# Residual norms of the second row tile in column halves, first loads reordered, waits for half the transposes, last norm interleaved

## The chip, the cores and the metric

One core of a Trainium2 chip runs the whole program as one launch. The metric is device time in microseconds (us). The kernel before took 3188.24 us (median of 3 runs, 3188.09 to 3198.32). Its profiled execution took 3180.1 us, of which the span of the core's instructions is 3178.1 us.

## The reference, cut to what matters

Two transformer stacks run one after the other on 256 tokens of width 1024, all in float32. The first has four layers, the second two.

```
first_block, layer i of 4 (kind = i % 3):
    q, k, v, ... = split(x @ w_in[kind]);  mix = attention of that kind;  mo = attention over memory rows
    x = layer_norm(ALPHA * x + concat(mix, mo) @ w_out[i])
    x = layer_norm(ALPHA * x + (silu(x @ w_gate) * (x @ w_up)) @ w_down)         # D_FF = 2816
second_block, layer i of 2:
    mix = mixer_ab(h) if i == 0 else mla(h)
    h = layer_norm(DN_ALPHA * h + mix)
    h = layer_norm(DN_ALPHA * h + mem_cross_attention(h, mem))
    h = layer_norm(DN_ALPHA * h + hier_moe(h))    # 32 experts of 1024 x 512 x 3 weights, 2 per token
layer_norm(x) = (x - mean) * rsqrt(var + eps) * g + b, over the 1024 columns
```

So there are fifteen norms with their gain and bias: one of the memory rows, twelve after a residual sum with a linear's output, and two after the experts.

## The kernel before, in words

The 256 rows are two tiles of 128 partitions, t = 0 and t = 1. The activations live in `x` (128 x 2 x 1024). TensorE (PE) takes them transposed, as `xT`, so each norm is followed by eight 128x128 transposes of a tile into PSUM (`trp`, two banks, four transposes a bank; function `x_columns`), and ScalarE (ACT) copies each bank to `xT`. `await_transposes` makes PE wait until all copies are done.

Weights come through a ring of 12 slots of 1 MB (`ring`), in the order in which SyncE (SP) issues them. PE frees a slot by an increment of `slots_used` at the last matmul that reads it, and SP, which waits in order, then issues the load twelve places on. In the expert stages six more slots in the arena join the ring, so 18 MB can be on their way; each stage reads 192 pieces of 1 MB.

The order on each engine is written out by hand; nothing is scheduled. Engines meet at semaphores. The places that matter here:

- The start: SP issues `ident`, `x` (both tiles in one DMA), the memory rows, the causal mask, two small tables and then the weights. PE waits for `ident` and `x`, does 16 transposes, waits for their copies, and starts the first projection (`linear_chunk`), whose weights are the first pieces in the ring.
- A residual norm (`add_and_normalise`, 12 of them): PE finishes tile 0 of a linear (`pe_for_vec`), goes on with tile 1, and puts tile 0's transposes shortly before tile 1's last matmuls. VectorE (DVE) adds PSUM to `x` over 1024 columns, does two `bn_stats` of 512 columns and one `bn_aggr`, asks GpSimd (POOL) for the inverse root, subtracts and multiplies by the gain meanwhile, waits for the root and does the last multiply-add, which ends in `ln_done`. It does the same for tile 1 when all the linear's slots are free (`slots_used >= complete`). Tile 1's transposes on PE stand behind whatever work can run without it.
- That work is: after the feed-forward of a layer (`ffn`), the next layer's first two chunks for tile 0 (`linear_by_tile`, four times); after attention in layers 0 to 2 and after `mla`, the next memory projection (`next_memory_kv`); after `mixer_ab`, a memory projection; after attention in layer 3, nothing; after cross attention (twice), only the router's small matmuls for tile 0 (`moe`).
- In `ffn` the down products of the last three of 11 units are held, so that tile 0 ends twelve matmuls before tile 1. For tile 1 they run unit by unit, the two 512-column halves of the output side by side.
- After the experts (`moe` on DVE) both tiles are normalised one after the other; after the last one SP writes `out` in one DMA.

## Time and profile before

| | |
|---|---|
| median of 3 runs | 3188.24 us |
| profiled execution | 3180.1 us |
| its span | 3178.1 us |
| PE busy (matmul) | 2769.9 us, 87% |
| DVE busy | 667.2 us, 21% |
| ACT busy | 382.4 us, 12% |
| POOL busy | 99.0 us, 3% |
| DMA, mean over the span | 221 GB/s |

The span cut in 40 slices shows two kinds of stages. In most slices PE is busy 90% or more and the DMA engines move 80 to 190 GB/s. In the two expert stages (slices 25 to 30 and 34 to 39) it is the other way round: about 420 GB/s, and PE at 60 to 80%. An engine's idle time costs something only where the engine that sets the end waits for it, so the rows below are read one place at a time: a view of idle times by releaser first, then the timeline around each place. In the rows a float32 matmul is recorded as two MATMUL rows, so x36 stands for 18 matmuls.

### The profile page before, as it was taken

How to read it: one execution, taken by the hardware profiler on the slowest of the kernel's cores; microseconds unless marked ns; L12 is line 12 of the kernel's file. 1: busy time of each engine (PE TensorE's matmuls, PEld its weight loads, DVE VectorE, ACT ScalarE, POOL GpSimd, SP SyncE). 2: the span in 40 equal slices, each digit the busy share in tenths (PEclk: the TensorE clock that was granted, in tenths of full speed). 3: DMA queues.
4: the chain of work that ended last, by engine and by line, in shares of the span. 5: the costliest groups of instructions: out<-in, count | busy, mean ns of one | idle time of the engine just before them, and what ended most of it. 6: DMA issues, size and time to landing. Idle time of an engine off the chain costs nothing.

```text
span 3178.1 us, 30120 instructions
## 1 busy us (share of the span) xinstructions
PE 2769.9 (87%) x12918; PEld 1655.7 (52%) x12918; DVE 667.2 (21%) x1611; ACT 382.4 (12%) x733; POOL 99.0 (3%) x48
## 2 busy tenths in 40 slices
PE   8999999999999999899999998766767998766664
PEld 4567755677457764577647775222223655322221
DVE  2610013000140013500155503100101323110111
ACT  1300002000120001300021112000000312000000
POOL 1000000000000000000000100000000000000000
PEclk9999999999999999999999998877788998888887
DMA  7344443544525444344423244999999435899996
GB/s 286 106 147 146 159 137 112 181 147 133 172 88 169 149 130 159 103 137 148 148 88 136 80 151 185 413 422 421 421 421 359 146 122 190 366 421 421 421 421 287
DMA packets 245464, 703.21 MB, mean 221 GB/s; under 512 B 18651, under 2 KB 119513, under 8 KB 195923
## 3 DMA queue, kind: packets, MB, share of 16 engines
q1 hardware_dynamic: 244032, 699.43, 58.8%
q8 instruction: 106, 1.74, 0.2%
q10 hardware_dynamic: 1299, 1.83, 0.2%
q14 instruction: 27, 0.22, 0.0%
HBM read 698.33 MB, written 1.05 MB: 220 GB/s over the span
## 4 chain that ended last, share of the span: by engine, by line
issue 73%; PE 13%; DMA 10%; POOL 2%; SPq 1%; DVE 1%; ACT 0%; ACTq 0%; POOLq 0%; DVEq 0%
PE sco L685 7%; PE lin L685 6%; DMA arena<-in_moe_w_down 3%; DMA arena<-in_moe_w_gate 3%; DMA ring<-in_moe_w_up 2%; DMA ring<-in_moe_w_gate 2%; DMA ring<-in_moe_w_down 2%; POOL roots L2003 2%; SPq L529 1%; PE trp L685 0%; PE trp L797 0%; ACT arena L1614 0%; DVE x L2071 0%; DVE arena L2637 0%; POOLq L179 0%
## 5 line engine op out<-in xcount | busy, mean ns | idle before, releaser
L685 PE MATMUL lin<-ring,arena 128*128 128x512 f32 (+4 forms) x3340 | 1183.2, 584 | 45.8 <-DMA arena<-in_moe_w_down 21.8
L685 PEld LDWEIGHTS lin<-ring,arena 128*128 128x128 f32 (+2 forms) x3340 | 518.5, 174 | 623.9 <-issue 597.2
L685 PE MATMUL sco<-arena,ring 128*128 128x256 f32 (+1 forms) x2836 | 621.5, 380 | 9.7 <-DVE arena L2594 9.0
L685 PEld LDWEIGHTS sco<-arena,ring 128*128 128x128 f32 x2836 | 541.5, 192 | 98.9 <-issue 16.7
L685 PE MATMUL sco<-ring,arena 128*32 128x512 f32 (+2 forms) x1428 | 276.8, 817 | 169.2 <-DMA ring<-in_moe_w_gate 89.2
L685 PE MATMUL sco<-arena 128*32 128x512 f32 (+6 forms) x1360 | 240.1, 595 | 95.4 <-DMA arena<-in_moe_w_gate 45.5
L685 PE MATMUL lin<-arena 128*128 128x128 f32 (+9 forms) x1632 | 257.7, 394 | 19.8 <-DMA ring<-in_moe_w_down 9.0
L685 PEld LDWEIGHTS sco<-ring,arena 128*32 128x32 f32 (+1 forms) x1428 | 79.5, 154 | 338.7 <-issue 334.7
L685 PEld LDWEIGHTS sco<-arena 128*32 128x32 f32 (+4 forms) x1360 | 103.7, 163 | 205.4 <-issue 189.9
L2240 DVE TENSOR_TENSOR arena<-arena,sco 128x256 f32<-128x256 f32 x88 | 37.1, 421 | 822.5 <-ACT arena L1701 822.5
L2003 POOL TENSOR_TENSOR roots<-roots 128x8 f32<-128x8 f32 x42 | 98.6, 2350 | 3072.8 <-DVE roots L2048 3044.5
L685 PEld LDWEIGHTS lin<-arena 128*128 128x128 f32 (+4 forms) x1632 | 144.0, 164 | 92.9 <-issue 68.2
L2655 DVE TENSOR_TENSOR arena<-arena,sco 128x512 f32<-128x512 f32 x16 | 11.0, 688 | 745.1 <-PE sco L685 745.1
L685 PE MATMUL lin<-arena,ring 128*128 128x256 f32 (+2 forms) x648 | 131.6, 385 | 3.6 <-issue 2.9
L1701 ACT ACTIVATE arena<-sco 128x256 f32<-128x256 f32 x88 | 33.8, 384 | 790.4 <-PE sco L685 790.4
L1614 ACT ACTIVATE arena<-trp 128x512 f32<-128x512 f32 (+1 forms) x123 | 67.0, 590 | 469.6 <-PE trp L797 466.9
L685 PEld LDWEIGHTS lin<-arena,ring 128*128 128x128 f32 (+1 forms) x648 | 108.8, 181 | 26.1 <-issue 7.3
L2082 DVE SCALAR_TENSOR_TENSOR x<-x,lin 128x1024 f32<-128x1024 f32 x24 | 29.3, 1222 | 217.2 <-PE lin L685 217.2
L685 PEld LDWEIGHTS trp<-arena 128*128 128x128 f32 x512 | 62.6, 203 | 16.6 <-issue 16.6
L685 PE MATMUL trp<-arena 128*128 128x128 f32 x512 | 65.6, 290 | 4.7 <-DVE arena L2637 4.7
L1605 ACT ACTIVATE arena<-lin 128x1024 f32<-128x1024 f32 (+3 forms) x36 | 32.9, 913 | 284.2 <-PE lin L685 284.2
L2167 DVE RECIPROCAL arena<-lin 128x256 f32<-128x256 f32 x34 | 59.7, 1756 | 9.4 <-PE lin L685 8.6
(249 smaller groups left out, 1116.3 us busy)
## 6 DMA issues: line engine op xcount, KB each, us to landing
ring<-in_moe_w_down SPq DMA_DIRECT2D x92, 1024.0 KB, 26.9
ring<-in_w_gate_up SPq DMA_DIRECT2D x88, 1024.0 KB, 5.1
ring<-in_moe_w_gate SPq DMA_DIRECT2D x88, 1024.0 KB, 26.9
ring<-in_moe_w_up SPq DMA_DIRECT2D x80, 1024.0 KB, 27.0
arena<-in_moe_w_up SPq DMA_DIRECT2D x48, 1024.0 KB, 26.7
ring<-in_w_down SPq DMA_DIRECT2D x44, 1024.0 KB, 4.8
arena<-in_moe_w_gate SPq DMA_DIRECT2D x40, 1024.0 KB, 27.2
arena<-in_moe_w_down SPq DMA_DIRECT2D x36, 1024.0 KB, 27.3
```

The costliest lines, as they stand in the source:

```text
L529: sp.dma_start(slot_rows(s).rearrange("p (k n) -> p k n", k=src.shape[1]), src).then_inc(slot_full[s], 16)
L685: return nc.tensor.matmul(o, lhsT, rhs, start=start, stop=stop)
L1605: nc.scalar.activation(dst[:, :, lo:lo + n], lin[:, pair:pair + 2, 0:n], ACT.Copy).then_inc(proj_done, 1)
L1614: nc.scalar.activation(dst, trp[0:rows, b, 0:n].rearrange("p (a b) -> p a b", a=shape[1]), ACT.Copy, scale=scale).then_inc(tr_done, 1)
L1701: nc.scalar.activation(silu_g[:, f, :], sco[:, f, 0:SEQ], ACT.Silu).then_inc(silu_done, 1)
L2003: nc.gpsimd.tensor_tensor(root_out[:, b, :], root_in[:, b, :], root_power, ALU.pow).then_inc(root_done, 1)
L2082: V.scalar_tensor_tensor(x[:, t, :], x[:, t, :], alpha, lin[:, 2 * t:2 * t + 2, :].rearrange("p a b -> p (a b)"), ALU.mult, ALU.add).then_ ...
L2167: V.reciprocal(pair_rinv, bank[:, SEQ:2 * SEQ]).then_inc(dve_step, 1)
L2240: V.tensor_tensor(hT[:, u % 4, f, :], silu_g[:, f, :], sco[:, f, SEQ:2 * SEQ], ALU.mult).then_inc(h_done, 1)
L2655: V.tensor_tensor(pair_h, pair_silu, sco[:, 1, :], ALU.mult).then_inc(h_done, 1)
```

## The change

Five things are changed.

1. Start. `x` comes in two DMAs, one a tile, with a semaphore of its own for tile 1; the first weight chunk (two slots) is issued right behind them, ahead of the memory rows, the mask and the small tables.
2. Residual norms of tile 1 (12). The add is cut in two halves of 512 columns, each with its `bn_stats` behind it; the first half starts when PE has finished that half's columns (two slots fewer than `complete`, or an extra increment of `pe_for_vec` in `ffn`), the second when all is done. For the latter, `ffn` does tile 1's held products half by half: all units for columns 0 to 511, then all units for the rest. Its three held slots are all freed in the second half.
3. Waits for half the transposes. In `linear_by_tile` and at the router, PE waits for the first of tile 1's two copies and does k = 0 to 3; before k = 4 it waits for the second.
4. The norms after the experts (2). Statistics and root requests of both tiles come first, then the two subtract-multiplies, then the two multiply-adds.
5. `out` is written in two DMAs, one a tile, each when its tile is done.

The core of the diff:

```diff
@@ -549,7 +549,9 @@
             sp.dma_start(ident[:, :], const("ident")).then_inc(x_loaded, 16)
-            sp.dma_start(x[:, :, :], A["x"][0].rearrange("(t p) d -> p t d", p=P)).then_inc(x_loaded, 16)
+            sp.dma_start(x[:, 0, :], A["x"][0, 0:P, :]).then_inc(x_loaded, 16)
+            sp.dma_start(x[:, 1, :], A["x"][0, P:2 * P, :]).then_inc(second_tile_loaded, 16)
+            load_chunk(A["w_in_a"][0], *FIRST_CHUNKS[0][0])
             sp.dma_start(memrows, A["mem"][0].rearrange("(t p) d -> p t d", p=P)).then_inc(input_loaded, 16)
@@ -557,7 +559,7 @@
                 w_in = (A["w_in_a"], A["w_in_b"], A["w_in_c"])[kind][j]
-                for c, n in FIRST_CHUNKS[kind][:3]:
+                for c, n in FIRST_CHUNKS[kind][int(layer == 0):3]:
                     load_chunk(w_in, c, n)
@@ -642,9 +644,10 @@
                 load_ln(A["ln3_g_2"][layer], A["ln3_b_2"][layer])
-            sp.wait_ge(ln_done, NT * LAYER_NORMS)
-            sp.dma_start(out[0].rearrange("(t p) d -> p t d", p=P), x[:, :, :]).then_inc(out_written, 16)
-            sp.wait_ge(out_written, 16)
+            for t in range(NT):
+                sp.wait_ge(ln_done, NT * LAYER_NORMS - NT + 1 + t)
+                sp.dma_start(out[0, t * P:(t + 1) * P, :], x[:, t, :]).then_inc(out_written, 16)
+            sp.wait_ge(out_written, 16 * NT)
         @block.tensor
@@ -734,9 +737,11 @@
                 between()
-                await_transposes()
+                await_transposes(1)
                 for i, (pair, n, w) in enumerate(head):
                     for k in range(kt):
+                        if i == 0 and k == 4:
+                            await_transposes()
                         last = mm(lin[:, pair + 1, 0:n], srcT[:, k, P:2 * P], w[k // 4][:, k % 4, :], start=k == 0, stop=k == kt - 1)
@@ -815,8 +820,8 @@
                     transposes([x[:, t, (b + j) * P:(b + j + 1) * P] for j in range(4)], free_slots if b == 0 else 0)
-            def await_transposes():
-                pe.wait_ge(tr_done, tr_items[0])
+            def await_transposes(but=0):
+                pe.wait_ge(tr_done, tr_items[0] - but)
             def cross_scores(h):
@@ -1002,12 +1007,17 @@
                 last.then_inc(pe_for_vec, 1)
-                for u in held:
-                    for f in range(2):
-                        if u == held[-1] and f == 1:
-                            x_columns(0)
-                        last = products(u, rows[u], f, 1)
-                    last.then_inc(slots_used, 1)
+                for n in range(2):
+                    for u in held:
+                        for f in range(2):
+                            if n == 1 and u == held[-1] and f == 0:
+                                x_columns(0)
+                            last = mm(lin[:, 2 + n, :], hT[:, u % 4, f, P:2 * P], rows[u][:, f, n * 512:(n + 1) * 512],
+                                      start=u + f == 0, stop=u == FFN_UNITS - 1 and f == 1)
+                        if n == 1:
+                            last.then_inc(slots_used, 1)
+                    if n == 0:
+                        last.then_inc(pe_for_vec, 1)
             def linear_columns(srcT, chunks, between=None, inside=None):
@@ -1303,9 +1313,11 @@
                         x_columns(1, 1)
-                        await_transposes()
+                        await_transposes(1)
                     o = sco[:, 0, t * 64:t * 64 + 36]
                     for k in range(KD):
+                        if t == 1 and k == 4:
+                            await_transposes()
                         mm(o, xT[:, k, t * P:(t + 1) * P], w[:, k, :], start=k == 0, stop=False)
@@ -1439,6 +1451,8 @@
             for t in range(NT):
+                if t:
+                    pe.wait_ge(second_tile_loaded, 16)
                 for b in range(0, KD, 4):
@@ -2062,6 +2076,11 @@
                 dve.wait_ge(dve_step, t_step.next())
+                scaled(rows, t, s, dst)
+
+            def scaled(rows, t, s, dst=None):
+
+                dst = rows if dst is None else dst
                 V.bn_aggr(mean_var[:, t, :], bn[:, t, :]).then_inc(dve_step, 1)
@@ -2071,18 +2090,33 @@
                                        ALU.mult, ALU.add).then_inc(ln_done, 1)
-            def add_and_normalise(alpha):
+            def add_and_normalise(alpha, projected=True):
                 complete = used.n
                 s = own_slot(2)
-                for t in range(NT):
-                    if t == 0:
+                dve.wait_ge(pe_for_vec, t_pe.next())
+                V.scalar_tensor_tensor(x[:, 0, :], x[:, 0, :], alpha, lin[:, 0:2, :].rearrange("p a b -> p (a b)"),
+                                       ALU.mult, ALU.add).then_inc(y_taken, 1)
+                dve.wait_ge(y_taken, t_taken.next())
+                normalise(x, 0, s)
+                for h in range(2):
+                    half = x[:, 1, 512 * h:512 * h + 512]
+                    if h == 1:
+                        dve.wait_ge(slots_used, complete)
+                    elif projected:
+                        dve.wait_ge(slots_used, complete - 2)
+                    else:
                         dve.wait_ge(pe_for_vec, t_pe.next())
+                    ins = V.scalar_tensor_tensor(half, half, alpha, lin[:, 2 + h, :], ALU.mult, ALU.add)
+                    if h == 0:
+                        ins.then_inc(dve_step, 1)
+                        dve.wait_ge(dve_step, t_step.next())
                     else:
-                        dve.wait_ge(slots_used, complete)
-                    V.scalar_tensor_tensor(x[:, t, :], x[:, t, :], alpha, lin[:, 2 * t:2 * t + 2, :].rearrange("p a b -> p (a b)"),
-                                           ALU.mult, ALU.add).then_inc(y_taken, 1)
-                    dve.wait_ge(y_taken, t_taken.next())
-                    normalise(x, t, s)
+                        ins.then_inc(y_taken, 1)
+                        dve.wait_ge(y_taken, t_taken.next())
+                    last = V.bn_stats(bn[:, 1, h * 6:h * 6 + 6], half)
+                last.then_inc(dve_step, 1)
+                dve.wait_ge(dve_step, t_step.next())
+                scaled(x, 1, s)
             def rotate(heads, cos, sin, half, scratch=rope_tmp, dst=None):
@@ -2690,8 +2724,22 @@
                 s = own_slot(2)
-                for t in range(NT):
-                    normalise(moe_sum, t, s, x)
+                rstd = []
+                for t in range(NT):
+                    for h in range(2):
+                        last = V.bn_stats(bn[:, t, h * 6:h * 6 + 6], moe_sum[:, t, h * 512:(h + 1) * 512])
+                    last.then_inc(dve_step, 1)
+                    dve.wait_ge(dve_step, t_step.next())
+                    V.bn_aggr(mean_var[:, t, :], bn[:, t, :]).then_inc(dve_step, 1)
+                    dve.wait_ge(dve_step, t_step.next())
+                    rstd.append(ask_root(mean_var[:, t, 1:2], ALU.add, LN_EPS))
+                for t in range(NT):
+                    ins = V.scalar_tensor_tensor(x[:, t, :], moe_sum[:, t, :], mean_var[:, t, 0:1], ring[:, s, 0:D], ALU.subtract, ALU.mult)
+                ins.then_inc(dve_step, 1)
+                dve.wait_ge(dve_step, t_step.next())
+                for t in range(NT):
+                    dve.wait_ge(root_done, t_root.next())
+                    V.scalar_tensor_tensor(x[:, t, :], x[:, t, :], rstd[t], ring[:, s, D:2 * D], ALU.mult, ALU.add).then_inc(ln_done, 1)
             V.memset(ones[:, :], 1.0).then_inc(dve_step, 1)
@@ -2794,7 +2842,7 @@
                 passed(3 * FFN_UNITS)
-                add_and_normalise(ALPHA)
+                add_and_normalise(ALPHA, False)
             for layer in range(SECOND_LAYERS):
```

On SP, at the start of the program. Before:

```order
L551 DMA ident<-in_consts 128x128
L552 DMA x<-in_x 128x2x1024
L553 DMA arena<-in_mem 128x2x1024
L554 DMA causal<-in_consts 128x512
L555 DMA small<-in_consts 128x8
L556 DMA ints<-in_positions 128x2
L448 DMA ring<-in_w_in_a 128x4x512 x2
L448 DMA ring<-in_w_in_a 128x4x328 x2
```

And now:

```order
L551 DMA ident<-in_consts 128x128
L552 DMA x<-in_x 128x1024
L553 DMA x<-in_x 128x1024
L448 DMA ring<-in_w_in_a 128x4x512 x2
L555 DMA arena<-in_mem 128x2x1024
L556 DMA causal<-in_consts 128x512
L557 DMA small<-in_consts 128x8
L558 DMA ints<-in_positions 128x2
L448 DMA ring<-in_w_in_a 128x4x328 x2
```

The two loads of the first weight chunk have moved ahead of four others, and `x` has become two loads.

On DVE, tile 1 of the norm behind the first attention (`x` and `lin` are the residual and PE's result, `small` the statistics, `roots` the inverse root). Before:

```order
L2082 SCALAR_TENSOR_TENSOR x<-x,lin 128x1024 [waits slots_used]
L2062 BN_STATS small<-x 128x6 [waits y_taken]
L2062 BN_STATS small<-x 128x6
L2065 BN_AGGR small<-small 128x2 [waits dve_step]
L2048 TENSOR_SCALAR roots<-small 128x1 [waits dve_step]
L2068 SCALAR_TENSOR_TENSOR x<-x,small,ring 128x1024
L2071 SCALAR_TENSOR_TENSOR x<-x,roots,ring 128x1024 [waits root_done,dve_step]
```

And now:

```order
L2109 SCALAR_TENSOR_TENSOR x<-x,lin 128x512 [waits slots_used]
L2116 BN_STATS small<-x 128x6 [waits dve_step]
L2109 SCALAR_TENSOR_TENSOR x<-x,lin 128x512 [waits slots_used]
L2116 BN_STATS small<-x 128x6 [waits y_taken]
L2084 BN_AGGR small<-small 128x2 [waits dve_step]
L2062 TENSOR_SCALAR roots<-small 128x1 [waits dve_step]
L2087 SCALAR_TENSOR_TENSOR x<-x,small,ring 128x1024
L2090 SCALAR_TENSOR_TENSOR x<-x,roots,ring 128x1024 [waits root_done,dve_step]
```

One add and one `bn_stats` of 512 columns now stand ahead of the wait for the linear's end.

On DVE, the last norm of the program (both tiles). Before:

```order
L2062 BN_STATS small<-arena 128x6 [waits slot_full6]
L2062 BN_STATS small<-arena 128x6
L2065 BN_AGGR small<-small 128x2 [waits dve_step]
L2048 TENSOR_SCALAR roots<-small 128x1 [waits dve_step]
L2068 SCALAR_TENSOR_TENSOR x<-arena,small,ring 128x1024
L2071 SCALAR_TENSOR_TENSOR x<-x,roots,ring 128x1024 [waits root_done,dve_step]
L2062 BN_STATS small<-arena 128x6 x2
L2065 BN_AGGR small<-small 128x2 [waits dve_step]
L2048 TENSOR_SCALAR roots<-small 128x1 [waits dve_step]
L2068 SCALAR_TENSOR_TENSOR x<-arena,small,ring 128x1024
L2071 SCALAR_TENSOR_TENSOR x<-x,roots,ring 128x1024 [waits root_done,dve_step]
```

And now:

```order
L2730 BN_STATS small<-arena 128x6 [waits slot_full6]
L2730 BN_STATS small<-arena 128x6
L2733 BN_AGGR small<-small 128x2 [waits dve_step]
L2062 TENSOR_SCALAR roots<-small 128x1 [waits dve_step]
L2730 BN_STATS small<-arena 128x6 x2
L2733 BN_AGGR small<-small 128x2 [waits dve_step]
L2062 TENSOR_SCALAR roots<-small 128x1 [waits dve_step]
L2737 SCALAR_TENSOR_TENSOR x<-arena,small,ring 128x1024 x2
L2742 SCALAR_TENSOR_TENSOR x<-x,roots,ring 128x1024 [waits root_done,dve_step]
L2742 SCALAR_TENSOR_TENSOR x<-x,roots,ring 128x1024 [waits root_done]
```

Tile 1's statistics have moved ahead of tile 0's two passes over the rows.

## Rows read from the trace of the kernel before

**Rows 1.** The page, part 1: busy time of each engine, share, instructions.

```profile
PE 2769.9 (87%) x12918; PEld 1655.7 (52%) x12918; DVE 667.2 (21%) x1611; ACT 382.4 (12%) x733; POOL 99.0 (3%) x48
```

**Rows 2.** Waits of PE over the span: releaser, us in total, times, longest.

```profile
PE trp L797 <- DVE x L2071: 17.6, 3, 7.2
PE lin L685 <- ACT arena L1614: 9.3, 11, 1.6
```

**Rows 3.** Stretches in the first expert stage: busy by engine, clock, DMA share, GB/s.

```profile
1980.00:1985.00 5.00, 4.31 (x41) 2.50 (x44) 0.00 (x0) 2.48 (x3) 0.00 (x0) 1.00 0.01 3
...
2010.00:2400.00 390.00, 252.95 (x1521) 89.60 (x1524) 39.11 (x114) 24.41 (x38) 0.00 (x0) 0.79 1.01 421
```

**Rows 4.** Timeline of the start: start, us, engine, line, operation, idle before.

```profile
6.47 3.78 PE L797 MATMUL trp<-ident,x 128*128 128x128 f32 x16 [6.47 <-DMA x<-in_x]
...
10.29 0.60 ACT L1614 ACTIVATE arena<-trp 128x512 f32<-128x512 f32 x1 [0.26 <-PE trp L797]
...
13.41 38.23 PE L685 MATMUL lin<-ring,arena 128*128 128x512 f32 x96 [3.16 <-DMA ring<-in_w_in_a]
```

**Rows 5.** DMA issues at the start: size, us from issue to landing.

```profile
x<-in_x SPq DMA_DIRECT2D x1, 1024.0 KB, 5.2
arena<-in_mem SPq DMA_DIRECT2D x1, 1024.0 KB, 7.4
```

**Rows 6.** Stretches where the clock changes; the column behind POOL is the clock.

```profile
13.00:14.00 1.00, 0.59 (x2) 0.37 (x3) 0.00 (x0) 0.00 (x0) 0.00 (x0) 0.94 1.05 389
...
17.00:18.00 1.00, 1.00 (x3) 0.38 (x2) 0.00 (x0) 0.00 (x0) 0.00 (x0) 0.85 1.07 374
...
1354.00:1356.00 2.00, 2.00 (x8) 1.65 (x7) 0.00 (x0) 0.00 (x0) 0.00 (x0) 0.67 0.00 0
```

**Rows 7.** Timeline, feed-forward of layer 0 into layer 1.

```profile
428.52 15.62 PE L685 MATMUL lin<-ring,arena 128*128 128x512 f32 x36
...
443.98 1.04 PE L797 MATMUL trp<-ident,x 128*128 128x128 f32 x8
...
444.61 1.09 ACT L1614 ACTIVATE arena<-trp 128x512 f32<-128x512 f32 x2 [15.24 <-PE trp L797]
...
445.75 2.84 PE L685 MATMUL lin<-ring,arena 128*128 128x512 f32 x6 [0.74 <-ACT arena L1614]
```

**Rows 8.** Timeline, tile 1 of the norm behind layer 3's attention.

```profile
1339.36 1.22 DVE L2082 SCALAR_TENSOR_TENSOR x<-x,lin 128x1024 f32<-128x1024 f32 x1 [7.45 <-PE lin L685]
...
1341.94 0.21 DVE L2065 BATCH_NORM_AGGREGATE small<-small 128x2 f32<-128x12 f32 x1
...
1346.47 1.97 PE L797 MATMUL trp<-ident,x 128*128 128x128 f32 x8 [7.15 <-DVE x L2071]
```

**Rows 9.** Timeline, second half of the router in the first expert stage.

```profile
1960.46 1.97 PE L797 MATMUL trp<-ident,x 128*128 128x128 f32 x8 [5.22 <-DVE x L2071]
...
1962.46 0.60 ACT L1614 ACTIVATE arena<-trp 128x512 f32<-128x512 f32 x1 [0.26 <-PE trp L797]
...
1963.11 3.63 PE L685 MATMUL sco<-ring,arena 128*128 128x36 f32 x16 [0.69 <-ACT arena L1614]
```

**Rows 10.** Timeline of the end.

```profile
3162.19 1.29 DVE L2062 BATCH_NORM_STATS2 small<-arena 128x6 f32<-128x512 f32 x2 [0.25 <-DVE arena L2645]
...
3163.99 2.60 POOL L2003 TENSOR_TENSOR roots<-roots 128x8 f32<-128x8 f32 x1 [479.55 <-DVE roots L2048]
...
3172.41 1.28 DVE L2071 SCALAR_TENSOR_TENSOR x<-x,roots,ring 128x1024 f32<-128x1024 f32 x1 [1.60 <-POOL roots L2003]
3173.73 0.40 SPq L646 DMA_DIRECT2D out<-x  x1
```

**Rows 11.** The DMA that writes the result: size, us to landing.

```profile
out<-x SPq DMA_DIRECT2D x1, 1024.0 KB, 4.0
```

**Rows 12.** DVE groups by shape: busy us, mean ns of one, idle before.

```profile
L2062 DVE BATCH_NORM_STATS2 small<-x 128x6 f32<-128x512 f32 x48 | 30.9, 685 | 0.8
...
L2465 DVE TENSOR_TENSOR arena<-arena,sco 128x512 f32<-128x512 f32 x16 | 11.0, 685 | 5.7 <-PE sco L685 5.6
```

More of the change, by code:

```diff
@@ L352, in build @@
         slots_used = sem("slots_used")
-        x_loaded, input_loaded = sem("x_loaded"), sem("input_loaded")
+        x_loaded, second_tile_loaded, input_loaded = sem("x_loaded"), sem("second_tile_loaded"), sem("input_loaded")
         proj_done = sem("proj_done")
```

## The prediction

> **What bounds the kernel now.** I read the page first: PE is busy 87% of the span, DVE, ACT and POOL far less [rows 1]. So outside the expert stages a microsecond counts only where PE stands still. Next the view of PE's waits, which gives the size of the prey. PE waits for a norm (DVE's last pass over x) 17.6 us in three places, and 9.3 us in eleven for ACT's copies of transposes [rows 2]. I went to each place in the timeline. The three waits for a norm are 7.15 us behind layer 3's attention [rows 8] and twice 5.2 us at the routers (what is left of the 17.6). In the other nine residual norms PE has other work until tile 1 is ready, so a shorter norm is worth nothing there.
>
> Then the stretches around the first expert stage. From 2010 to 2400 the DMA engines move 421 GB/s at full share, so the stage lasts as long as its weights. But ahead of it, from 1980 to 1985, they move 3 GB/s at 1% share [rows 3]: the slots are full, and the loads go on only when PE frees the first. The stage's end thus moves with PE's start, as long as that hole is not used up. The ends of the program are chains of their own: PE waits for x at the start [rows 4], and DVE, POOL and one DMA run alone at the end [rows 10].
>
> **The start.** Before, x lands at 1.19 + 5.2 = 6.4 us, the 16 transposes begin at 6.47, the last copy ends at 10.29 + 0.60 = 10.89, and PE then waits until 13.41 for weights [rows 4, 5]. The memory rows land at 1.66 + 7.4 = 9.06, so 1 MB takes 2.66 us here [rows 5]. Now tile 0 is half of x and lands 1.3 us earlier, at 5.1; tile 1 lands at 6.4 as before, sooner than PE has finished tile 0. The transposes shift as a block, and the last copy ends at 9.6. The first weight piece follows x and lands at 6.4 + 2.7 to 2.9 = 9.1 to 9.3. PE starts at 9.64 instead of 13.41: 3.8 us. The second piece lands near 12, and eight matmuls on the first take over 7 us. The memory rows' norm waits for its gain and bias, which stay behind the same number of bytes, and PE comes to it only after the 38 us of matmuls in rows 4.
>
> The clock comes on top. At 13.41 it was at its full 2.4 GHz; it fell to half at 13.9 and returned at 17.3 (0.94 and 0.85 are the means over 13 to 14 and 17 to 18 [rows 6]). Ahead of the fall PE had been idle since 10.25. That stretch cost 3.4 / 2 = 1.7 us. In the new order PE pauses only about 0.7 us between transposes and matmuls. I take it that the clock comes up at about 10.5, as it must have before, since nothing ran between 10.25 and 13.41, and doesn't fall: 0.4 us lost instead of 1.7. Start: 3.8 + 1.3 = 5.1 us. If the clock comes up only behind a stretch of matmuls as long as the one that ended at 17.3 (3.9 us), 1.9 us are lost instead of 1.7 and the start gives 3.5. A late return (6.2 us, as behind layer 3) would leave 2.4. If PE never falls and is fast at once, 5.5.
>
> The Trainium skill bears on just this. "TensorE: Matmul & The Clock Gate", Part 4 (PE-mode transpose), says that transposes do not count as work for the clock. By that rule the start would be worth the 3.5 above. Here the trace speaks against it, as the clock was full at 13.41 with nothing but transposes before [rows 6].
>
> **Waits for half the transposes.** In linear_by_tile the transposes end at 443.98 + 1.04 = 445.02, the second copy at 445.70, and PE goes on at 445.75, 0.74 us later [rows 7]. A copy takes 0.60 [rows 9], so the first ends at 445.21, and PE can go on at 445.26: 0.49 us. Four matmuls of 0.86 us (18 in 15.62 [rows 7]) cover the second copy. Four such places: 2.0 us. At a router the copies are 0.85 us apart at the half clock: the first is done before PE's last transpose ends (1960.46 + 1.97 = 1962.4), and the matmuls start at 1963.11 [rows 9]: 0.65 us each, 1.3 for two. Between them the four matmuls take 0.9, as 16 rows of k take 3.63; the second copy ends at 1963.06, in time.
>
> **Column halves.** Behind PE's last matmul DVE now adds 512 columns instead of 1024 and does one bn_stats instead of two. Before, from the add's start to bn_aggr: 1341.94 - 1339.36 = 2.58 us [rows 8]. Now an operation of 512 columns from PSUM takes 0.69 and a bn_stats 0.69 [rows 12], with two hand-overs of 0.03: 1.43. Gain 1.15 us where PE waits: layer 3 and two routers, 3.45 us. In the other nine places nothing. The first half's add costs nothing, since DVE idles until PE's end (7.45 us in rows 8). The idle of PE shrinks from 7.15 to 6.0, so the clock, which was at half there and came back at 1355.3 (0.67 over 1354 to 1356 [rows 6]), will still fall; how soon it returns varies between the 3.4 us at the start and 6.2 here. I put 0.3 us for it, with -0.5 and +1.4 as ends; the gathers at the two routers, which lie across the same rise, -1 to +1.
>
> **The expert stages** pass on what the router gains (0.65 + 1.15 = 1.8 us each), because the hole of over 5 us in the DMA stream [rows 3] stays open. The norm of the first expert stage is followed by a memory projection on PE, so its interleaving gives nothing.
>
> **The end.** Before, bn_stats begins at 3162.19, the last pass ends at 3172.41 + 1.28 = 3173.69 [rows 10]. Now: root 0 runs on POOL from 3163.99 as before; tile 1's statistics end at about 3165.4, the two subtract passes (1.28 each) at 3168.0, the first multiply-add at 3169.3. Root 1 can start only when root 0 is through, at 3166.6, and is done at 3169.2, just in time; the last pass ends at 3170.6. Gain 3.1 us. The result's 1 MB takes 4.0 us from issue to landing [rows 11]; at 1 MB in 2.66 us, half of it is 1.3 us shorter, and tile 0's half is under way by then: 1.2 us. End: 4.3 us, with 3.1 as the lower end if two DMAs finish no sooner than one.
>
> **Held products and slots.** By halves, ffn's held matmuls are as many as before, and each has its own weight load either way. The first held slot comes free after 8 of 12 matmuls instead of 4, 3.4 us later, the second 1.7. The load that takes it is used only after four chunks, over 40 us of PE's work. Cost nothing.
>
> **Sum.** 5.1 + 2.0 + 1.3 + 3.45 + 0.3 + 4.3 = 16.4 us. 3180.1 - 16.4 = 3163.7 for the profiled execution. That lay 0.26% under the median of the runs; scaled to 3188.24 it is 3172. In ratio 0.9948.
>
> **Rivals.**
> A. The clock at the start behaves as in the second case, and layer 3's return falls badly (-0.5): the sum is 14.0, and the time 3174. For it speaks that the first 16 transposes ran at the slow pace, 3.78 us, while 8 take 1.04 at the full clock and 1.97 at half [rows 4, 7, 8]; against it the full clock at 13.41. The Trainium skill's rule on transposes, cited above, is for this case.
> B. The clock comes back early at layer 3 (+1.4) and the gathers gain: 18 to 19 us, 3169.
> C. The expert stages swallow everything ahead of them, since they end with their DMA. Then only the last norm and the result are left: 4.3 us, 3184. Against it stands the hole at 1% share [rows 3], which must be gone for this; it holds where the DMA stream starts at a time of its own.
> D. Slower: the later slots. Loads go out in order, so each of the four feed-forward ends would push all loads behind it by 3.4 us. If PE came to the next layer's chunk just as it lands, it would wait 3.4 us four times, and each such idle would bring down the clock (1.7 to 3.1 us more): 20 to 26 us, against 16 gained. The kernel would be 4 to 10 us slower, 3192 to 3198. It decides once a load has under 3.4 us to spare. Only waits of PE for weights in the first four layers would speak for it, and I found one alone, at 13.41 [rows 4].
> E. The new order of loads does not hold PE's start earlier, because the two weight pieces land with the rest: the start gives 1.3 (tile 0) or nothing, sum 11 to 12.5, 3176.
>
> **Chances.** The forecast 0.40, A 0.27, B 0.13, C 0.05, D 0.04, E 0.11. A measurement of this kernel tells about 0.5% (16 us) from no change, and the forecast lies right on that line. Faster by over 0.5% are a bit over half of the forecast's own and B, and a share of A by the spread of the runs, 0.42; within 0.5% the rest with C and E, 0.54; slower by over 0.5% hardly D, 0.04. The range: B's end below and C above are 3169 and 3184, and the runs before spread by 10 us, which I add below in part: 3162 to 3184.
>
> **What would show it.** Start: first transposes at 5.1, first matmul at 9.6, clock not at half after 11. linear_by_tile: a gap of 0.2 to 0.3 us instead of 0.74. Layer 3: 6.0 us of idle; routers: 4.1 us, then no 0.69 us gap. Expert stage: the hole in the DMA stream a bit shorter, 421 GB/s as before, its end earlier by all that came before it. End: last pass 8.4 us after the first bn_stats instead of 11.5. Wrong if the hole is gone, if PE waits for weights in layers 1 to 3, or if POOL's second root ends later than the second subtract pass.

## The result, and the profile after

| us | before | after |
|---|---|---|
| median of the runs, five each | 3188.24 (3188.09 to 3198.32) | 3172.54 (3167.57 to 3176.57) |
| profiled execution | 3180.1 | 3170.12 |
| its span | 3178.1 | 3168.3 |
| mean granted clock of the span | 0.931 | 0.930 |

The ratio is 0.9939, with a 95% interval of 0.9918 to 0.9959: the kernel is faster by about 0.6%. A repetition of the same two kernels (e6_again below) gave 0.9968, 0.9949 to 0.9987. In that session the 23 runs of before fell into two groups, 13 at 3177.8 to 3180.8 us and 10 at 3193.9 to 3197.4, so a median depends on how many of each a session has. The means of all runs differ by 19.6 us in the first session (3191.9 and 3172.3) and by 12.2 in the repetition (3186.7 and 3174.5). The median came out where the prediction had it. The profiled execution did not: it gained 10.0 us where the sum said 16.4. The last part of this section is about that difference.

The places are read as before, one at a time. The start, in the timeline (columns: start, us, engine, line, operation, idle before), answers to [rows 4]:

```profile
4.95 3.56 PE L802 MATMUL trp<-ident,x 128*128 128x128 f32 x16 [4.95 <-DMA x<-in_x]
...
9.19 36.56 PE L688 MATMUL lin<-ring,arena 128*128 128x512 f32 x96 [0.69 <-ACT arena L1628]
```

The DMA issues of the start, for [rows 5]:

```profile
x<-in_x SPq DMA_DIRECT2D x2, 512.0 KB, 4.1
arena<-in_mem SPq DMA_DIRECT2D x1, 1024.0 KB, 11.0
```

The first matmul is at 9.19 instead of 13.41 (4.2 us), and its group of 96 rows takes 36.56 instead of 38.23 (1.7 us). The wait for weights, 3.16 us before, is gone; PE waits 0.69 us for a copy. Together 5.9 us, where the prediction had 5.1.

linear_by_tile between layers 0 and 1, for [rows 7]:

```profile
438.08 1.04 PE L802 MATMUL trp<-ident,x 128*128 128x128 f32 x8
438.71 1.09 ACT L1628 ACTIVATE arena<-trp 128x512 f32<-128x512 f32 x2 [15.24 <-PE trp L802]
439.36 1.98 PE L688 MATMUL lin<-ring,arena 128*128 128x512 f32 x4 [0.25 <-ACT arena L1628]
```

The wait is 0.25 us instead of 0.74, so 0.49, as forecast. The norm behind layer 3's attention, for [rows 8]:

```profile
1333.96 0.69 DVE L2109 SCALAR_TENSOR_TENSOR x<-x,lin 128x512 f32<-128x512 f32 x1 [6.12 <-PE lin L688]
1334.69 0.69 DVE L2116 BATCH_NORM_STATS2 small<-x 128x6 f32<-128x512 f32 x1
1335.42 0.21 DVE L2084 BATCH_NORM_AGGREGATE small<-small 128x2 f32<-128x12 f32 x1
...
1339.96 1.97 PE L802 MATMUL trp<-ident,x 128*128 128x128 f32 x8 [6.03 <-DVE x L2090]
1342.61 9.75 PE L688 MATMUL sco<-arena,ring 128*128 128x256 f32 x36 [0.69 <-ACT arena L1628]
```

From the last add's start to `bn_aggr` it is 1.46 us instead of 2.58, and PE stands still for 6.03 instead of 7.15. The clock comes back sooner too. Stretches of 2 us (columns: stretch, length, busy time by engine, then behind POOL the clock, DMA share, GB/s), for the last row of [rows 6]:

```profile
1344.00:1346.00 2.00, 2.00 (x6) 1.59 (x5) 0.00 (x0) 0.00 (x0) 0.00 (x0) 0.50 0.40 162
1346.00:1348.00 2.00, 2.00 (x10) 1.74 (x10) 0.00 (x0) 0.00 (x0) 0.00 (x0) 0.97 0.00 0
```

It is at 1.2 GHz up to 1346 and at 2.4 GHz from there, 3.5 us behind the first matmul at 1342.61, where before it took 6.2. The first router, second half, for [rows 9]:

```profile
1958.38 1.97 PE L802 MATMUL trp<-ident,x 128*128 128x128 f32 x8 [4.10 <-DVE x L2090]
1960.19 3.63 PE L688 MATMUL sco<-ring,arena 128*128 128x36 f32 x16
...
1968.73 2.35 PE L688 MATMUL sco<-arena,ring 128*128 128x32 f32 x10 [4.48 <-DVE arena L2628]
1973.42 5.79 PE L688 MATMUL trp<-arena 128*128 128x128 f32 x32 [2.35 <-DVE arena L2671]
1979.90 1.50 PE L688 MATMUL sco<-ring,arena 128*32 128x512 f32 x12 [0.69 <-ACT arena L1887]
```

The wait for the norm is 4.10 us instead of 5.22 and the 0.69 behind the transposes is gone. From the router's first matmul to the experts' first it is 27.7 us here and was 29.4; at the second router 27.6 and was 30.2. The two waits give 1.8 us at each; the rest is the gather of the routed rows (`trp<-arena`), 5.79 us for 5.54 at the first router and 5.67 for 6.31 at the second. The rows in between show what is still left: 4.48, 2.35 and 0.69 us of idle, and matmuls at half pace. In the expert stage the hole in the DMA stream stands as before, and behind it the 421 GB/s, for [rows 3]:

```profile
1979.00:1984.00 5.00, 4.31 (x42) 1.35 (x45) 0.00 (x0) 1.88 (x2) 0.00 (x0) 1.00 0.01 3
2010.00:2400.00 390.00, 253.74 (x1524) 89.47 (x1524) 39.07 (x114) 23.36 (x37) 0.00 (x0) 0.79 1.01 421
```

The end, for [rows 10, 11]: DVE, POOL and SyncE in the timeline, and the DMA that writes the result (size, us to landing).

```profile
3156.85 1.29 DVE L2730 BATCH_NORM_STATS2 small<-arena 128x6 f32<-128x512 f32 x2 [0.25 <-DVE arena L2679]
3158.65 4.24 POOL L2017 TENSOR_TENSOR roots<-roots 128x8 f32<-128x8 f32 x2 [477.85 <-DVE roots L2062]
3160.11 2.47 DVE L2737 SCALAR_TENSOR_TENSOR x<-arena,small,ring 128x1024 f32<-128x1024 f32 x2
3162.62 2.48 DVE L2742 SCALAR_TENSOR_TENSOR x<-x,roots,ring 128x1024 f32<-128x1024 f32 x2
3163.93 1.53 SPq L649 DMA_DIRECT2D out<-x  x2
```

```profile
out<-x SPq DMA_DIRECT2D x2, 512.0 KB, 2.7
```

From the first `bn_stats` to the last pass's end it is 8.25 us and was 11.50; from there to the span's end 3.2 and was 4.4. That is 4.45 us, against 4.3 forecast.

**Where the other microseconds went.** I took the start of tile 0's residual add at each of the twelve norms in both traces. The distance between the two traces is how far the kernel after is ahead at that point: 5.9 us at the first and second norm, 4.4 at the third and fourth, 4.9 at the fifth and sixth, 5.4 at the seventh, 7.9 at the eighth, 1.0 at the ninth and tenth, 2.5 at the last two, then 5.3 at the last norm and 9.8 at the end. It should never fall, and it falls twice: by 1.5 us between the second and the third (layer 1's attention), and by 6.9 between the eighth and the ninth (`mixer_ab`). The second of these stretches, before and after:

```profile
1569.74:1805.67 235.93, 224.21 (x1363) 156.47 (x1362) 136.13 (x223) 43.31 (x74) 15.76 (x8) 0.96 0.26 89
```

```profile
1561.88:1804.71 242.83, 231.94 (x1363) 162.65 (x1362) 136.58 (x223) 43.50 (x74) 15.76 (x8) 0.92 0.25 87
```

PE has the same 1363 matmul rows and DVE the same 136 us. Only the clock differs, 0.96 and 0.92. With one linear_by_tile in it the stretch should have become 0.5 us shorter, and it is 6.9 longer. Layer 1's attention, before and after, tells the same in small (clock 0.99 and 0.97):

```profile
419.30:547.30 128.00, 122.18 (x485) 66.14 (x484) 38.02 (x96) 25.23 (x43) 5.22 (x2) 0.99 0.45 130
```

```profile
413.40:542.90 129.50, 123.77 (x485) 66.81 (x484) 38.19 (x98) 25.11 (x43) 5.22 (x2) 0.97 0.43 128
```

So 7.4 us were lost to the clock in one place and 2.0 in the other. 9.8 + 7.4 + 2.0 = 19.2 us is, as an estimate, what the change would have given in this execution with before's clock there, more than the 16.4 of the sum. What no single pair of traces can say is whether the change itself brings the clock down there. The experiments were made for that; they show that it can come down there without the change, and leave open whether the change makes it more frequent.

### The profile page after: what moved, and what is told of

Same layout as the page of the kernel before. It is cut to its first block, busy times and chain, and to the rows that moved or that the text cites. A ratio compares the mean times of both kernels' runs of the same rounds, so it can differ in the third digit from the quotient of the medians.

```text
span 3168.3 us, 30133 instructions
## 1 busy us (share of the span) xinstructions
PE 2778.5 (88%) x12918; PEld 1661.7 (52%) x12918; DVE 669.5 (21%) x1623; ACT 382.2 (12%) x733; POOL 97.0 (3%) x48
## 4 chain that ended last, share of the span: by engine, by line
issue 58%; DMA 20%; PE 16%; SPq 3%; POOL 2%; DVE 1%; ACT 0%; ACTq 0%; POOLq 0%; DVEq 0%
PE sco L688 9%; PE lin L688 6%; DMA ring<-in_moe_w_down 4%; DMA ring<-in_moe_w_gate 4%; DMA arena<-in_moe_w_down 4%; DMA arena<-in_moe_w_gate 4%; DMA ring<-in_moe_w_up 3%; SPq L529 3%; POOL roots L2017 2%; DMA arena<-in_moe_w_up 1%; PE trp L688 0%; PE trp L802 0%; DVE x L2090 0%; DVE arena L2671 0%; ACT arena L1628 0%
## 5 line engine op out<-in xcount | busy, mean ns | idle before, releaser
L2671 DVE TENSOR_SCALAR arena<-arena 128x32 f32<-128x32 f32 x256 | 54.4, 298 | 7.3 <-PE lin L688 7.2
```

Of the source, the lines that this page charges most:

```text
L2671: ins = V.tensor_scalar(dst[:, t, PLACES * j:PLACES * j + PLACES], places, place_of[:, t, column], weight[:, t, column], ALU.is_equal, ALU ...
```

## The experiments

Each of the first four has one part of the change alone (e4_end has two), on the kernel before. Shifts below are distances to the profile of before, at the same marks as above.

**e1_start: the start alone.**

```diff
-            sp.dma_start(x[:, :, :], A["x"][0].rearrange("(t p) d -> p t d", p=P)).then_inc(x_loaded, 16)
+            sp.dma_start(x[:, 0, :], A["x"][0, 0:P, :]).then_inc(x_loaded, 16)
+            sp.dma_start(x[:, 1, :], A["x"][0, P:2 * P, :]).then_inc(second_tile_loaded, 16)
+            load_chunk(A["w_in_a"][0], *FIRST_CHUNKS[0][0])
```

> Only part 1 of the change (x in two loads, first weight chunk ahead of the memory rows). In the changed kernel's profile the first norm stood 5.9 us earlier than before, 4.2 of it from the first matmul (9.19 for 13.41) and 1.7 from a clock that no longer falls to half. Theory: this part gives the 5.9 by itself, and every later norm keeps the 5.9 except where the granted clock changes; I expect the clock in mixer_ab to differ from the profile of before, since PE arrives there at another time, so the shift at the norm behind mixer_ab lies anywhere between 0 and 10 us. Rival: something else in the change (the halves in the feed-forward, or the later slots) causes the 2 us lost in layer 1 and the 7.4 us lost in mixer_ab; then this kernel keeps 5.9 us there. Time against before: theory 0.997 to 0.999, rival 0.998.

Measured: median 3183.82 (3171.84 to 3193.1) over ten runs, 3179.9 for the kernel before beside it, ratio 0.9994 with 0.9968 to 1.0019. So the timed comparison says nothing, and its runs spread by 21 us. The profile (span 3175.0) says more: the shift is 3.2 to 3.3 us at all twelve norms. Its start:

```profile
5.21 3.83 PE L799 MATMUL trp<-ident,x 128*128 128x128 f32 x16 [5.21 <-DMA x<-in_x]
9.73 38.70 PE L687 MATMUL lin<-ring,arena 128*128 128x512 f32 x96 [0.69 <-ACT arena L1618]
```

```profile
9.80:13.00 3.20, 3.20 (x4) 1.44 (x5) 0.00 (x0) 0.00 (x0) 0.00 (x0) 1.00 1.05 404
```

And the same stretch in the kernel after, which has the same start:

```profile
9.80:13.00 3.20, 3.20 (x9) 1.45 (x8) 0.00 (x0) 0.00 (x0) 0.00 (x0) 1.00 1.04 402
```

PE goes on 3.7 us sooner than before, as predicted, but runs 4 rows in the 3.2 us where the kernel after runs 9: half pace, up to 14.1 in its timeline. The first 96 rows take 38.70 us instead of 36.56. The recorded clock reads 1.00 in both. So the position term (3.8) holds, and the clock term behind it is no constant: +1.7 in the kernel after, -0.5 here. e6_again and f1_fill, with the same order of loads, took 36.56 us again, and f2_fill_rwkv 38.23, so three of the five profiles with this start were at full pace from the first matmul.

The theory of this run failed in two places. The start did not give 5.9 us by itself, and the clock in `mixer_ab` did not differ although PE came there 3.3 us sooner: 235.91 us at a clock of 0.96, as before, and layer 1's attention lost nothing either. By the text above that speaks for its rival, that another part of the change has a share in the two losses. The next three runs bear on that.

**e2_halves: the column halves alone.**

```diff
+                for h in range(2):
+                    half = x[:, 1, 512 * h:512 * h + 512]
...
+                    ins = V.scalar_tensor_tensor(half, half, alpha, lin[:, 2 + h, :], ALU.mult, ALU.add)
...
+                    last = V.bn_stats(bn[:, 1, h * 6:h * 6 + 6], half)
```

> Only part 2 (column halves in the residual norms, held products by halves). Theory: nothing at the nine covered norms, 1.15 us of DVE work less at layer 3 and at each router; with the clock's return behind layer 3 the shift of the next norm is 1.1 to 2.8 us. 1.1 us at each router. Rival: the held products or the late slots cost: then norms 1, 3, 5, 7 (behind the feed-forwards) stand later than before, or the mixer_ab stretch is 7 us longer by waits that are not at half clock.

Measured: one run, 3187.34, which is no gain. In the profile nothing shifts up to the seventh norm (0.0 to 0.1 us), which also rules out rival D: the later slots cost nothing. In the kernel after, too, PE waits for no weights but those of the experts. At the eighth the kernel is 2.3 us ahead, through layer 3:

```profile
1345.29 1.97 PE L797 MATMUL trp<-ident,x 128*128 128x128 f32 x8 [6.03 <-DVE x L2081]
```

The idle is 6.03 us, as in the kernel after. Of the 2.3 us, 1.1 is that, and the rest is the clock's sooner return, which need not be the change's doing: e4_end, whose program is that of before up to there, gained 1.0 us at this place. Then `mixer_ab` takes 12.3 us more than before (248.2 us, clock 0.90 against 0.96), and the shift is -10. Both routers' waits are 4.10 us here too, and the routers take 28.9 and 28.1 us instead of 29.4 and 30.2. But from the tenth to the eleventh norm, across the first expert stage, the shift grows by only 0.1 us, and from the twelfth to the last by 2.5.

**e3_half_waits: the half waits alone.**

```diff
-                await_transposes()
+                await_transposes(1)
...
+                        if i == 0 and k == 4:
+                            await_transposes()
```

> Only part 3 (PE waits for one of two copies, then for the other before k = 4). Theory: 0.49 us at each of four places and 0.65 at each router. Norms 2 to 3 stand 0.5 us earlier than before, 4 and 5 1.0, 6 1.5, and behind mixer_ab 2.0 give or take the clock. Rival: the wait before k = 4 costs PE a pause of its own, so the gain is under 0.3 a place.

Measured: one run, 3190.48. The shifts go up by 0.5 us at each linear_by_tile (-1.88, -1.39, -0.93 at norms three, five and seven), as predicted. Layer 1's attention takes 1.9 us off before that, `mixer_ab` 12.1 behind it (247.5 us at 0.90; the wait gained in each stretch is counted back in). A third kernel, then, whose edit touches only one wait in these stretches, and it loses there. At the routers the 0.69 us behind the transposes is gone, and the routers take 28.2 and 29.6 us instead of 29.4 and 30.2. The rival is out: no pause before k = 4 takes the gain away.

**e4_end: the last norms and the split write alone.** Up to the first experts' norm its program is word for word that of before.

```diff
+            for t in range(NT):
+                sp.wait_ge(ln_done, NT * LAYER_NORMS - NT + 1 + t)
+                sp.dma_start(out[0, t * P:(t + 1) * P, :], x[:, t, :]).then_inc(out_written, 16)
```

> Only parts 4 and 5 (interleaved norms behind the experts, result in two DMAs). Theory: the last pass ends 8.25 us behind the first bn_stats instead of 11.5, and the span's end 3.2 us behind that instead of 4.4: 4.5 us in all, nothing in layer 1 of the second stack. Up to the last expert stage the run is the kernel before, so the norms' times up to there differ from its profile only by the clock: they show how much two runs of the same program differ. If they agree within 0.1 us everywhere, the clock's course is fixed by the program and not by the run; rival: mixer_ab differs by several us between two runs of the same code.

Measured: one run, 3192.41, of which the end itself is right: 8.2 us from the first `bn_stats` (3178.71) to the last pass's end (3186.95), 3.2 from there to the span's end at 3190.1. But at the ninth norm, up to which nothing differs, it is 14.8 us behind before. The stretch of `mixer_ab`:

```profile
1570.32:1820.48 250.16, 239.05 (x1363) 167.34 (x1362) 136.56 (x223) 43.41 (x74) 15.75 (x8) 0.89 0.24 84
```

The same instructions took 235.93 us in one execution and 250.16 in another, with the clock at 0.96 and 0.89. Layer 1's attention, too, lost 1.4 us here. So neither loss needs the change. That the change has no share in them is not shown: of the four profiles whose program up to there differs from before's in nothing but the first loads (before, e1_start, e5_weights_first, e4_end), three took 235.9 us at 0.96 and one 250.2; of the five with the column halves or the half waits and no filler in `mixer_ab` (e2_halves, e3_half_waits, after, e6_again, f1_fill), none took under 242.8. With one execution each that can be chance, and no run here decides it. The kernel loses another 1.5 us between the tenth and the eleventh norm, where the expectation had nothing: 0.9 of it in the router (30.3 us for 29.4), and the rest is not taken apart.

**e5_weights_first: the first weight chunk behind x, x in one DMA.**

```diff
             sp.dma_start(x[:, :, :], A["x"][0].rearrange("(t p) d -> p t d", p=P)).then_inc(x_loaded, 16)
+            load_chunk(A["w_in_a"][0], *FIRST_CHUNKS[0][0])
```

> The kernel before with one edit: the first weight chunk is issued right behind x, which stays one load. Theory: the first matmul waits only for the last copy of a transpose, so it stands at 10.9 instead of 13.41; the other 1.3 us of the start need x in two loads. The first norm stands 2.5 us earlier than before, plus or minus 1.7 for the clock at the start. Rival: the weights still land with the rest (in order of their bytes, but not sooner than 12), then 1 us or less.

Measured: one run, 3177.4. The first matmul is at 10.64, 2.8 us sooner than before, and the shift is 2.5 to 2.8 us at all twelve norms:

```profile
6.18 3.77 PE L798 MATMUL trp<-ident,x 128*128 128x128 f32 x16 [6.18 <-DMA x<-in_x]
10.64 38.48 PE L686 MATMUL lin<-ring,arena 128*128 128x512 f32 x96 [0.69 <-ACT arena L1615]
```

So of the start's 4.2 us, 2.8 are the order of the loads and the rest the halving of x: 1.4 by the kernel after, 0.9 by e1_start, whose first matmul is at 9.73. Rival E is out.

**e6_again: the kernel after once more**, beside the two that follow, on the same chip.

> The changed kernel once more, unaltered. Theory: from run to run only the stretches with a clock at half differ (start, layer 1's attention, the feed-forward of layer 3, mixer_ab, the routers), so this profile's norms differ from the first one's by the half-clock time alone, up to 2 us in layer 1 and up to 10 us in mixer_ab, and its timed runs spread over 10 us or more, as those of the kernel before do (3177.6 to 3196.7). Against before 0.994 to 0.997. Rival: the changed kernel has one course of its own, with 7 us lost in mixer_ab in each run; then the profile agrees with the first within 0.5 us.

Measured: median 3175.28 (3162.97 to 3181.87, twelve runs) against 3180.73, ratio 0.9968, 0.9949 to 0.9987. With before's two groups of runs (above), the first session's 15.7 us and this one's 5.5 can both be true measurements of one change. The profile is ahead by 5.7, 5.9, 6.4 and 6.9 at norms two, three, five and seven, 8.5 at the eighth, and 2.9 behind at the ninth. That is not the course of the first profile: layer 1's attention lost 0.3 us here (2.0 there), `mixer_ab` 11.8 (7.4 there), and layer 3 gave 1.6 (2.5 there). So the rival is out. What the two profiles share is that `mixer_ab` lost.

**f1_fill: the kernel after, with matmuls in PE's idle time** at layer 3's norm and at the routers. Their products go to a PSUM bank that is free there. In the diff's order the four calls stand at the router ahead of tile 1's transposes, ahead of the routing result and ahead of the first gather, and in layer 3 ahead of tile 1's transposes.

```diff
+            def keep_busy(n, bank=None, width=512):
+                for _ in range(n):
+                    mm((lin[:, 0, :] if bank is None else bank)[:, 0:width], ident[:, :], x[:, 0, 0:width])
...
+                        keep_busy(4)
...
+                keep_busy(5)
...
+                keep_busy(2)
...
+                    keep_busy(6)
```

> The changed kernel, with matmuls of no use (the identity with 512 columns of tile 0 of x, into a PSUM bank that is free) in PE's idle time: six ahead of tile 1's transposes in layer 3, four ahead of tile 1's transposes at each router, five ahead of the routing result, two ahead of the first gather. They take 0.86 us each at full clock and fit in the idle stretches (6.0, 4.1, 4.5 and 2.4 us). Theory: the clock stays at 2.4 GHz through these places; behind layer 3 the first expert matmuls of the feed-forward are no longer slow (2.4 to 3.5 us), and at each router the transposes (1.97 to 1.04), 16 narrow matmul rows (3.6 to 1.9), ten more (2.3 to 1.2) and the gather (5.5 or 6.3 to 4.0) give 5 to 6 us. Together 13 to 15 us faster than the changed kernel, 0.9955 of it. Rival: the clock falls all the same, or the fillers push the transposes back: then 0 or slower by up to 3 us.

Measured: median 3161.4 (3155.17 to 3164.84, six runs), ratio to before 0.9933, 0.9911 to 0.9955; 13.9 us under e6_again beside it, and 13.3 in the two spans (3158.6 and 3171.9). It is the fastest kernel here. Layer 3 in its timeline:

```profile
1332.76 5.31 PE L688 MATMUL lin<-x,ident 128*128 128x512 f32 x12
1338.95 1.09 PE L802 MATMUL trp<-ident,x 128*128 128x128 f32 x8 [0.89 <-DVE x L2099]
1340.78 9.55 PE L688 MATMUL sco<-arena,ring 128*128 128x256 f32 x43 [0.74 <-ACT arena L1637]
```

The 6.03 us of idle are filled but for 0.89, the eight transpose rows take 1.09 instead of 1.97, and in the next 9.6 us PE does 43 rows where the kernel after did 36 in 9.75. The first router:

```profile
1955.60 3.68 PE L688 MATMUL lin<-x,ident 128*128 128x512 f32 x8
1959.87 1.09 PE L802 MATMUL trp<-ident,x 128*128 128x128 f32 x8 [0.59 <-DVE x L2099]
1961.21 1.98 PE L688 MATMUL sco<-ring,arena 128*128 128x36 f32 x16 [0.25 <-ACT arena L1637]
...
1972.29 3.81 PE L688 MATMUL trp<-arena 128*128 128x128 f32 x32 [1.28 <-DVE arena L2680]
1976.78 1.50 PE L688 MATMUL sco<-ring,arena 128*32 128x512 f32 x12 [0.69 <-ACT arena L1896]
```

The gather takes 3.81 us (5.79), the router's 16 rows 1.98 (3.63), and experts begin 23.1 us behind the router's first matmul, against 27.7 after and 29.4 before. Against e6_again, at the same marks, f1_fill gains 3.4 us at layer 3, nothing in `mixer_ab` (247.85 and 247.24 us), 7.1 from the ninth to the eleventh norm and 3.9 from there to the end. Of the 7.1, 4.5 are the router's (27.6 us in e6_again, 23.1 here); the second router, too, takes 23.1 us for 27.6. The rest of the 7.1 is another thing than the filled waits. Ahead of the memory projection behind the first experts' norm, PE stands still for 2.9 to 3.0 us in all eight profiles without fillers, released by nothing that the profile shows ("issue"), and the 64 rows behind it take 15.74 us. In f1_fill and f2_fill_rwkv the pause is not there, and the rows take 13.98. Nothing on record says why; smaller losses elsewhere take a part of it back. The clock theory is shown for the three filled places, with 12.4 us together, and not for all of the 13.9.

**f2_fill_rwkv: f1_fill, with fillers in mixer_ab too.**

```diff
+                        if h > 1:
+                            keep_busy(1, trp[:, 0, :], 256)
...
+                    keep_busy(1, trp[:, 0, :])
```

> The same, and in mixer_ab a filler of 256 columns ahead of each of six waits of the stage with 64-row matmuls, and one of 512 columns behind its 64-column matmuls, for each tile. Theory: they cost 1 to 3 us a tile and keep the clock up where it falls in most runs (9 to 27 us at half clock lost between the norms 7 and 8), so the median is 5 us under f1_fill and the spread of the runs shrinks from 15 to under 8 us. Rival: the fall comes elsewhere in mixer_ab (levels with waits for DVE and ACT) and the fillers only cost: 2 to 6 us slower than f1_fill.

Measured: median 3164.5 (3153.72 to 3183.47, twelve runs), ratio 0.994, 0.9917 to 0.9962: no better than f1_fill, and its runs spread wider. The stretch of `mixer_ab` took 253.7 us against 247.85 in f1_fill, in one execution of each (f2_fill_rwkv, then f1_fill):

```profile
1559.30:1813.00 253.70, 244.87 (x1390) 166.93 (x1389) 136.81 (x223) 43.50 (x74) 15.75 (x8) 0.93 0.24 83
```

```profile
1558.35:1806.20 247.85, 237.29 (x1363) 166.99 (x1362) 136.49 (x223) 43.52 (x74) 15.75 (x8) 0.90 0.24 85
```

The clock rose from 0.90 to 0.93, worth about 5 us at the slope worked out below, and the fillers cost more than that. PE is busy 7.6 us longer there (244.87 for 237.29), while its idle time in the stretch shrank by only 1.7 us (8.8 for 10.6). So most of the fillers' time did not fall into pauses. That they delay a chain in which PE is waited for is my reading, and no run takes it apart.

## Why the prediction was right, and where it was not

**What bounds the kernel.** Right. Nothing in the expert stages swallowed the gain ahead of them: the hole at 3 GB/s stayed, and the shift grew over each such stage, by 1.6 and 2.8 us. In e1_start the 3.2 us of the start came through both stages. Rival C is out. How much of a router's gain gets through is not as steady as the prediction had it: in e2_halves the first stage passed on 0.1 us.

**Start, 5.1 forecast, 5.9 found.** The position part was 4.2 us for 3.8. The clock part was 1.7 for 1.3 in the profile, but -0.5 in e1_start with the same order of loads. So rival A described something real, as one of two courses and not as the rule. The Trainium skill's "TensorE: Matmul & The Clock Gate", Part 4 (PE-mode transpose), says that transposes don't count as work for the clock. In the kernel after, PE was at full pace from 9.19 with only transposes behind it, which speaks against the rule; in e1_start it was not, which fits it. As f1_fill and f2_fill_rwkv have the same instructions at the start and went different ways (36.56 and 38.23 us), the rule alone does not tell the outcome, and no run here shows what does.

**Half waits, 2.0 and 1.3 forecast.** 0.49 at linear_by_tile, as forecast, and the whole gap of 0.69 at the router, for 0.65; e3_half_waits has them alone.

**Column halves, 3.45 + 0.3 forecast.** The idle shrank by 1.12 us at each of the three places. Behind layer 3 the clock came back 3.5 us after PE's first matmul and not 6.2, so layer 3 gave 2.5 us instead of 1.45 (in the kernel after; 2.3 in e2_halves). That was the first half of rival B in these two executions. In e6_again layer 3 gave 1.6, near the forecast, and e4_end gained 1.0 there with no change at all, so the term was rightly put as a range, and which end of it a profile shows is luck. The routers gave 1.7 and 2.6 us locally, where 1.8 each was forecast; the difference is the gathers, inside the 1 us either way that was allowed for them.

**End, 4.3 forecast, 4.45 found.** Its working was off inside: a root was put at 2.6 us, and two back to back took 4.24. I had also named as a sign of failure that the second root ends after the second subtract pass. It does, at 3162.89 against 3162.58, and costs nothing, since the pass that needs it starts at about 3163.9. The sign was set one pass too early, and the prediction's own times already had it so: the second root done at 3169.2, the second subtract pass at 3168.0.

**The step that failed** is the one under the sum: "3180.1 - 16.4 = 3163.7 for the profiled execution." It took everything that the change doesn't touch to last as long as before. Two such stretches lost 9.4 us, with the same instructions but for one wait, through a lower clock. Over before, after, e4_end, e6_again and f1_fill, `mixer_ab`'s length is 235.9, 242.8, 250.2, 247.2 and 247.9 us, at clocks 0.96, 0.92, 0.89, 0.90 and 0.90. The time at half clock is twice length times (1 - clock), as a stretch wholly at 1.2 GHz has a mean of 0.50: an estimate of 18.9, 38.9, 55.0, 49.4 and 49.6 us, so that each microsecond at half clock costs 0.34 to 0.40. The profile of before was at the fast end of this, with e1_start and e5_weights_first, and the prediction read from it as though it were the kernel's own. That the median of the first session nevertheless met the forecast is partly luck: the repetition gave a third of it. Both intervals lie under 1, and the forecast's 0.9948 lies between the two ratios, 0.9939 and 0.9968.

**What stays open.** What makes the clock take one course or the other in `mixer_ab`, in layer 1's attention, behind layer 3 and in the first 18 us, with the same instructions. Whether the column halves and the half waits make the slow course of `mixer_ab` more frequent: profiles of several executions of both kernels would tell. And whether the clock can be held in `mixer_ab` by fillers that cost less.

## What to carry to other kernels

Trace each part of a change at marks through the program, not only in the total: here every local gain was right within 1.1 us while the total of one profile was off by 6. Before a change of half a per cent is believed or doubted, look whether some stretch that it does not touch has changed its clock, and in more than one profile of the kernel before, as the one that a forecast starts from can be a lucky one. Where PE must stand still for 5 us for another engine, a few matmuls into a spare PSUM bank gave more (3.4 to 4.5 us at each of three places) than shortening the wait had (1.6 to 2.6). There they ended before what PE waits for, with 0.59 us or more to spare ahead of the transposes.

## What the runs showed of the hardware

- The granted clock in one long stretch of small matmuls (`mixer_ab`) had a mean of 0.89 to 0.96 in nine executions with the same 1363 rows on PE, and the stretch took 235.9 to 250.2 us. Three of them, whose PE came there at times up to 3.3 us apart, agree within 0.1 us.
- In e1_start the recorded clock read 1.00 while PE did four 512-column rows in 3.2 us; in the kernel after it did nine at the same reading. At the start of a trace, the rows' own pace has to be looked at.
- Behind layer 3 the clock came back 3.5 us after PE's first matmul in the kernel after and 6.2 us after it in the kernel before.
- With the idle time filled, the clock stayed at 2.4 GHz. The first line is f1_fill over 1330 to 1350, the second the kernel after over 1332 to 1352:

```profile
1330.00:1350.00 20.00, 18.38 (x70) 12.22 (x69) 4.64 (x7) 2.75 (x4) 2.61 (x1) 1.00 0.47 158
```

```profile
1332.00:1352.00 20.00, 13.28 (x49) 10.15 (x48) 4.27 (x7) 2.86 (x4) 2.61 (x1) 0.83 0.48 156
```
